# Moving the sample value pages, the sample value products and ten top-k rounds in a two-layer hybrid decoder step

## The reference, cut to what matters

```python
# layer 0, sample group: one query token for each of 8 samples, 1024 past positions + itself
score = einsum(relu(qi . idx_keys), wi) * IDX_SCALE      # indexer, 8 heads
_, idx = lax.top_k(score, 256)                           # prompt: top_k(score, 128) over <= 512 keys
k_sel, v_sel = gather from cache_k / cache_v by page_table (pages of 128 rows), new k, v for the last
logits = q . k_sel * ATTN_SCALE + t5_bias(table, dist)   # 16 heads, 4 KV heads
p = softmax(logits);  out = p . v_sel;  x = LN(ALPHA * x + out @ w_out)
# then a squared-ReLU MLP (4096), then layer 1: banded attention (window 128) with sinks, then an MLP
```

## Time and profile before

| what | value |
| --- | --- |
| median of 3 runs | 1299.87 us (1298.53 to 1301.01) |
| profiled execution, its own time | 1300.45 us |
| its span | 1298.8 us |
| PE busy | 1215.7 us (94%) |
| DVE busy | 708.2 us (55%) |
| ACT busy | 473.8 us (36%) |
| POOL busy | 102.0 us (8%) |

### The profile page before, as it was taken

One profiled execution on the slowest core, in us unless ns is written; L12 is line 12 of the kernel. 1 busy time (PEld: TensorE's weight loads), 2 busy tenths in 40 slices (PEclk: granted clock), 3 DMA queues, 4 the chain that ended last, 5 costly groups with the idle time before them and its releaser, 6 DMA issues.

```text
span 1298.8 us, 25590 instructions
## 1 busy us (share of the span) xinstructions
PE 1215.7 (94%) x9573; PEld 1113.3 (86%) x9573; DVE 708.2 (55%) x1440; ACT 473.8 (36%) x863; POOL 102.0 (8%) x139
## 2 busy tenths in 40 slices
PE   8999866999999999999999897889999999999995
PEld 4948723569999999999999896579999999999995
DVE  2289963766764343343357915957833433433477
ACT  2342214763452232231234426744531322322332
POOL 4333430000004000000000210000000000000000
PEclk9989968999999999999999998999999999999998
DMA  6645696002122222222223231012122222222221
GB/s 199 188 144 179 227 288 197 2 1 98 66 66 87 92 97 82 97 97 81 97 88 124 57 97 50 33 50 98 50 98 86 92 98 81 97 96 82 97 82 66
DMA packets 62155, 129.99 MB, mean 100 GB/s; under 512 B 9995, under 2 KB 34483, under 8 KB 61954
## 3 DMA queue, kind: packets, MB, share of 16 engines
q1 hardware_dynamic: 40978, 107.15, 24.3%
q10 hardware_dynamic: 14944, 13.91, 3.5%
q0 software_dynamic: 6160, 7.94, 2.2%
HBM read 124.35 MB, written 9.79 MB: 103 GB/s over the span
## 4 chain that ended last, share of the span: by engine, by line
PE 75%; DVE 16%; ACT 3%; SPq 3%; issue 3%; DMA 1%; POOL 0%; ACTq 0%; DVEq 0%
PE PS L541 59%; PE PS L571 6%; PE PS L761 2%; PE PS L721 2%; PE PS L708 2%; PE PS L735 2%; DVE YA L1521 2%; SPq L371 1%; DVE PB L1657 1%; SPq L362 1%; DVE YA L1508 1%; DVE PB L1682 1%; DVE RSTD L1513 1%; ACT PB L1133 1%; DVE X L1527 1%
## 5 line engine op out<-in xcount | busy, mean ns | idle before, releaser
L1364 DVE TENSOR_TENSOR WLO<-WRAW,WHI 128x1024 fp32r<-128x1024 f32 x118 | 145.3, 1232 | 352.5 <-ACT WHI L966 352.4
L966 ACT ACTIVATE WHI<-WRAW 128x1024 fp32r<-128x1024 f32 x126 | 133.5, 1060 | 404.2 <-PE PS L541 385.7
L541 PE MATMUL PS<-XH,WHI 128*128 128x260 f32 x1344 | 273.1, 284 | 1.9 <-DVE XL L1689 1.6
L541 PE MATMUL PS<-XH,WLO 128*128 128x260 f32 x1344 | 271.4, 284 | 0.0
L541 PE MATMUL PS<-XL,WHI 128*128 128x260 f32 x1344 | 270.8, 283 | 0.0
L541 PEld LDWEIGHTS PS<-XH,WHI 128*128 128x128 f32 x1344 | 207.7, 189 | 3.3 <-DVE XL L1689 2.3
L541 PEld LDWEIGHTS PS<-XH,WLO 128*128 128x128 f32 x1344 | 207.8, 189 | 0.0
L541 PEld LDWEIGHTS PS<-XL,WHI 128*128 128x128 f32 x1344 | 207.2, 189 | 0.0
L541 PE MATMUL PS<-HH,WHI 128*128 128x260 f32 x896 | 181.4, 283 | 0.2 <-DVE HL L1388 0.2
L541 PE MATMUL PS<-HH,WLO 128*128 128x260 f32 x896 | 180.6, 283 | 0.0
L541 PE MATMUL PS<-HL,WHI 128*128 128x260 f32 x896 | 180.3, 283 | 0.0
(11 more groups left out here) (268 smaller groups left out, 1732.1 us busy)
## 6 DMA issues: line engine op xcount, KB each, us to landing
WRAW<-wall SPq DMA_DIRECT2D x168, 512.0 KB, 3.2
bias_skewed<-bias_seq ACTq DMA_DIRECT2D x4, 1280.0 KB, 6.8
BT<-bias_skewed ACTq DMA_DIRECT2D x4, 1024.0 KB, 16.2
X<-xT SPq DMA_DIRECT2D x4, 520.0 KB, 7.2
X<-xT SPq DMA_DIRECT2D x1, 2080.0 KB, 10.2
yT<-X SPq DMA_DIRECT2D x8, 260.0 KB
KVB<-cacheK SPq DMA_DIRECT2D x16, 128.0 KB, 2.7
KVX<-cacheK SPq DMA_DIRECT2D x16, 128.0 KB, 3.0
```

Source lines behind the costliest of these rows:

```text
L541: mm = pe.matmul(PS[:, 2 * slot + g, 0:TG], w[:, slot, k, :], x[:, k, TG * g:TG * g + TG], start=(k == 0 and w is WHI and x is hi), stop=( ...
L966: nc.scalar.activation(WHI[:, slot], WRAW[:, slot], ACT.Copy).then_inc(hi_done, 1)
L1364: V.tensor_tensor(WLO[:, slot], WRAW[:, slot], WHI[:, slot].bitcast(F32), ALU.subtract).then_inc(lo_dve, 1)
```

## The change

It gives V pages their own places, brings the blocks of the prompt's masks and the first bias block elsewhere, and gives four queues a new order. PE does logits(0) and logits(1) of the prompt before the sample value products; the products move into the hook `sample_a(-1)`, their banks from 4 and 5 to 6 and 7, and the sample output's transposes to iteration 0, its copies (ACT and DVE) to iteration 1. DVE does 4 rounds (not 8) ahead of the query copies and 6 (not 5) behind them; the last ten stand between softmax_in(1) and normalise(0). The copies of the queries are cut in three, and the K logits run `gp` outermost, so that the first half needs the first four query units only. The new V row is multiplied straight out of `NAT` by an 8-row probability matrix that one more DVE operation (`DG`) and one matmul prepare. High and low parts of units 14 and 15 are made in iterations 3 and 4, since V pages stand in `WHI` and `WLO`. The digit matmuls sit one slot later each, the last three two slots later. Skewing the bias (four 1280 KB transfers) goes from ACT in units 8 to 11 to SP in the time of unit 5.

```diff
-KV_PLACE = (9, 10, 7, 8, 0, 1, 2, 3, 4, 5, 6, 9, 10, 7, 8, 11)
+KV_PLACE = (9, 10, 7, 8, 0, 1, 2, 3, 4, 5, 6, 12, 13, 11, 14, 9)
...
-KV_SPLIT = ((8, 8), (8, 8), (8, 8), (0, 8), (8, 8), (8, 8), (0, 8), (0, 8),
-            (4, 6), (4, 6), (4, 6), (5, 7), (5, 7), (5, 7), (5, 7), (4, 6))
-V_ORDER = (8, 9, 10, 15, 11, 12, 13, 14)
+KV_SPLIT = ((8, 8), (8, 8), (0, 0), (0, 8), (8, 8), (8, 8), (0, 8), (0, 8),
+            (4, 6), (4, 6), (4, 6), (4, 6), (8, 8), (4, 6), (4, 6), (4, 6))
+V_LATE = (8, 9, 10, 11, 13, 14, 15)
...
-SLOT_OF = (1, 2, 3, 4, 5, 6, 7, 8, 10, 11, 12)
+SLOT_OF = (2, 3, 4, 5, 6, 7, 8, 9, 12, 13, 14)
...
+        def load_values(eng, q, numbers):
+
+            eng.wait_ge(unit_done, A_OUT)
+            for n in V_LATE:
+                if kv_before(n):
+                    eng.wait_ge(kv_used, kv_before(n))
+                load_sample(eng, q, n, numbers)
...
+            early(POOL_LO[0] // 2, 0)
+            sp.wait_ge(toe_out, 16)
+            for i0 in range(0, P, 32):
+                sp.dma_start(bass.AP(tensor=bskew.tensor, offset=i0 * (NH * SKEW + 1),
+                                     ap=[[NH * SKEW + 1, 32], [SKEW, NH], [1, 640]]),
...
+            numbers = page_numbers(sp, 0, V_LATE)
+            early(POOL_LO[0] // 2, 1)
+            sp.wait_ge(toe_skew, 16 * 4)
+            sp.wait_ge(is_relu, 3 * IDXH)
             sp.wait_ge(ds_mm, 3)
-            with sp.Fori(0, NPG) as pg:
-                load_page(sp, 2, pg)
+            sp.dma_start(BT0[:], bskew[:, :, 127 + 384:127 + 512]).then_inc(toe_in[0], 16)
...
-            load_values(sp, 0)
+            sp.wait_ge(mask_done, 1)
+            sp.wait_ge(outs, 16 * 2)
+            with sp.Fori(0, NPG) as pg:
+                load_page(sp, 12, pg)
+            load_values(sp, 0, numbers)
             sp.wait_ge(kv_used, 2 * DB)
+            sp.wait_ge(toe_in[3], 16)
+            sp.wait_ge(lo_pool, LO_SKIP)
             for s in range(2):
                 load_unit(POOL_LO[1] + s, s)
...
-            with pool.Fori(0, NPG) as pg:
+            with pool.Fori(0, 4) as pg:
                 load_page(pool, 3, pg)
-            for u in range(*POOL_LO):
+            for u in range(POOL_LO[0], A_OUT):
                 low_part(u, u % 2)
...
+                if u < POOL_LO[0] + 4:
+                    load_page(pool, 3, 4 + u - POOL_LO[0])
+            load_values(pool, 1, numbers)
+            for u in range(A_OUT, POOL_LO[1]):
+                low_part(u, u % 2)
...
+            pe.wait_ge(ds_ev, 1)
+            for c0, c1 in spans:
+                pe.matmul(PSF[:, 2048 + c0:2048 + c1], TREP[:], ohd[:, c0:c1], start=True,
+                          stop=False)
             pe.wait_ge(qb_ready, 1)
...
+            for gp in range(2):
+                if gp:
+                    pe.wait_ge(qb_ready, 2)
+                for quad in (range(0, 4), range(4, 8)):
...
+            def sample_values():
+
+                pe.wait_ge(d_p, 1)
                 for k in range(NPG):
+                    pe.transpose(PS[:, 4 + k // 4, (k % 4) * P:(k % 4 + 1) * P],
+                                 PD[:, k * P:(k + 1) * P], ident)
+                pe.wait_ge(dg_done, 1)
...
                 if i == -1:
+                    sample_values()
+                if i == 0:
+                    pe.wait_ge(ov_ev, 2)
                     for q in range(2):
...
+                    numbers = page_numbers(act, 2, V_LATE)
...
-                high_part(u + 2, u % 2)
+                if u + 2 < A_OUT:
+                    high_part(u + 2, u % 2)
...
+                if 6 <= u < 8:
+                    with act.Fori(4 * (u % 2), 4 * (u % 2) + 4) as pg:
+                        load_page(act, 2, pg)
...
+            load_values(act, 2, numbers)
...
             act.wait_ge(d_mx, 1)
             nc.scalar.activation(PD[:], PD[:], ACT.Exp, bias=DST[:, 1:2],
                                  accum_out=DST[:, 2:3]).then_inc(d_exp, 1)
+            act.wait_ge(toe_skew, 16 * 4)
+            act.wait_ge(kv_used, DB)
+            load_bias(1)
...
                 if i == -1:
+                    for q in range(2):
+                        act.wait_ge(kv_used, DB + 4 * q + 4)
+                        nc.scalar.activation(OV[:, q, :], PS[0:112, 6 + q, 0:256], ACT.Copy
+                                             ).then_inc(ov_ev, 1)
+                    load_bias(2)
+                    load_bias(3)
+                if i in (3, 4):
+                    high_part(A_OUT + i - 3, i - 3)
+                if i == 1:
                     act.wait_ge(do_mm, 1)
...
-            prompt_rounds(8)
-            dve.wait_ge(ev_act, A_OUT)
...
+            prompt_rounds(4)
             dve.wait_ge(z_qb, 2)
...
+            dve.wait_ge(ev_act, 10)
+            queries(0, 4).then_inc(qb_ready, 1)
+            dve.wait_ge(ev_act, A_OUT - 1)
+            queries(4, 7)
+            dve.wait_ge(ev_act, A_OUT)
+            queries(7, 8).then_inc(qb_ready, 1)
+            prompt_rounds(6)
...
             prompt_rounds(1)
             sample_normalise(1, PD[:], False)
-            prompt_rounds(len(left))
+            dve.wait_ge(d_p, 1)
+            V.tensor_scalar(DG[:], ident, PD[:, 1024:1025], None, ALU.mult).then_inc(dg_done, 1)
 
             def sample_a(i):
 
                 if i == -1:
+                    prompt_rounds(len(left))
+                if i == 1:
                     dve.wait_ge(do_hi, 1)
```

More of the change, by code:

```diff
@@ L234, in program @@
         KID = place("KID", [P, 5, 2, HD])
+        KVZ = place("KVZ", [P, NPG, 256], at=kw)
         KIT = place("KIT", [P, TOK])
@@ L240, in program @@
         SC = place("SC", [P, 3, 512], at=ww)
+        MK12 = place("MK12", [P, 640], F32R, at=ww + 1536)
+        MK3 = place("MK3", [P, 512], F32R, at=hw + 7600)
         RS = place("RS", [P, 2, 512], at=ww + 1536)
@@ L277, in program @@
         DST = place("DST", [P, 4])
-        PNEW = place("PNEW", [1, P])
+        PNEW = place("PNEW", [DB, P])
         YS = place("YS", [P, TOK], at=rw)
@@ L386, in load_index_page, with page_numbers, load_sample @@
                           ).then_inc(done, 16)
-        def load_values(eng, q):
-            for group in (V_ORDER[:4], V_ORDER[4:]):
-                pages = {n: [page_number(eng, n, pg) for pg in range(*kv_pages(n)[q])]
-                         for n in group}
-                eng.wait_ge(unit_done, A_OUT)
-                for n in group:
-                    if n == 15:
-                        eng.wait_ge(lo_pool, LO_SKIP)
-                    if kv_before(n):
-                        eng.wait_ge(kv_used, kv_before(n))
-                    for pg, page in zip(range(*kv_pages(n)[q]), pages[n]):
-                        fetch_page(eng, n, pg, page)
+        def page_numbers(eng, q, samples):
+            return {n: [page_number(eng, n, pg) for pg in range(*kv_pages(n)[q])]
+                    for n in samples}
+        def load_sample(eng, q, n, numbers):
+            for pg, page in zip(range(*kv_pages(n)[q]), numbers[n]):
+                fetch_page(eng, n, pg, page)
+        def load_values(eng, q, numbers):
[4 more added lines that the diff above has]
+                load_sample(eng, q, n, numbers)
+        masks = (MK0[:], MK12[:, 0:256], MK12[:, 256:640], MK3[:])
         turns_a = Turns(lambda t: (0, t + 1))
@@ new lines, in sample_values @@
+            def sample_values():
+                pe.wait_ge(d_p, 1)
+                for k in range(NPG):
+                    pe.transpose(PS[:, 4 + k // 4, (k % 4) * P:(k % 4 + 1) * P],
+                                 PD[:, k * P:(k + 1) * P], ident)
+                pe.wait_ge(dg_done, 1)
+                pe.matmul(PS[0:DB, 6, 0:P], CST[:, C_SAM:C_SAM + DB], DG[:],
+                          start=True, stop=True).then_inc(dt_mm, 1)
+                pe.wait_ge(dt_ev, 1)
+                for b in range(DB):
+                    pe.matmul(sample_out(b), PNEW[:, NH * b:NH * b + NH],
+                              NAT[0:DB, 4, HD + IDXH:NATW], start=True, stop=False)
+                for quad in (range(0, 4), range(4, 8)):
+                    for b in quad:
+                        wait_kv(DB + b)
+                    for k in range(NPG):
+                        for b in quad:
+                            mm = pe.matmul(sample_out(b), PTD[:, k, NH * b:NH * b + NH],
+                                           kv_place(DB + b)[:, k, :], start=False,
+                                           stop=(k == NPG - 1))
+                            if k == NPG - 1:
+                                mm.then_inc(kv_used, 1)
```

157 lines of the change are left out of this document (61 added, 96 removed).

## The result

The changed kernel takes 1280.38 us (median of 4 runs, 1278.51 to 1280.54), the kernel before took 1300.44 beside it (4 runs, 1298.53 to 1302.15): a ratio of 0.9843 [0.9826, 0.9860], 20.1 us less. Forecast were 1275.0 us and 24.6 less, so the gain came, and 4.5 us of it are missing. The profiled executions say the same: spans of 1298.8 and 1278.8 us. From the start of unit 14 to the end both take 1004.3 us, so the whole difference lies ahead of it.

What follows compares the result with a forecast made beforehand. DMA engines (V pages), then an uncovered serial chain, were taken to set TensorE's first turn of probabilities. 30.7 - 0.6 - 5.5 = 24.6 us off 1300.45 gives 1275.9, predicted as 1275 us; forecast 1271 to 1278, range 1268 to 1283.

Steps and rivals of the forecast that it cites:

- Step 2: K logits on TensorE: start right behind unit 13 without idle at full clock, take 8.8 us, end at about 160.
- Step 5: Attention from first turn to unit 14: added work hands back 5.5 us, 3.2 of it a wait for the sample output's copies.
- step 3: VectorE's chain from the mask at 145.7 sets the next point: first probabilities scaled at 188.2, 30.7 us earlier.
- Step 4: Whether TensorE is free by the first scaling: V complete between 177 and 184, 0.6 us put on the path (bounds 0 and 5).
- step 1: Units 6 to 13 on TensorE with later digit slots: unit 13 ends near 150.3, 6.3 us earlier (bounds 4 and 7.5).
- the rival of the value path: V comes at 184 or later, with the bias load amid its pages: 1280 us (1278 to 1285), chance 0.18.
- unit 13 after 153: Sign on TensorE's timeline: unit 13 ending later than 153 us would make the units 6 to 13 estimate wrong.
- Count one of the two: VectorE's digit chain: one of two slow operations beside GpSimd's low parts assumed to go, some 2 us.
- a wait beyond 190: Sign on TensorE's timeline: waiting for V pages or a bias load beyond 190 us would make the prediction wrong.
- The rival of 150 GB/s: V pages and bias load run at half the rate seen: 10 us slower, 1310 us, chance 0.03.
- the 3 us more: Under the attention: by the exclusive port lock, VectorE's scalings and GpSimd's low parts exclude each other, sum some 3 us worse.
- the 30.7 us: First probabilities scaled by VectorE at 188.2 instead of 218.86 us: the gain before deductions.

Runs made afterwards that it cites:

- Experiment 5: The changed kernel with the digit matmuls back in their old slots (1 to 8, 10 to 12): 1281.45 us, ratio 0.9844 to the kernel before.
- Experiment 2: The changed kernel with SP reading V sample 12's page numbers ahead and issuing its eight pages straight, not in a loop: 1278.83 us.
- experiment 1: The changed kernel with ScalarE asking for the 2 MB of bias block 1 behind the first two exponentials instead of ahead of them: 1275.81 us.
- experiment 3: The changed kernel with VectorE taking the sample output's low part in iteration 2, between normalise(2) and softmax_in(4), instead of iteration 1: 1275.81 us.
- Experiment 4: The changed kernel with sample value products ahead of logits(0) again and the ten top-k rounds ahead of softmax_in(0): 1288.39 us.
- experiment 6: The changed kernel with high parts, and so low parts, of units 14 and 15 in iterations 6 and 7 instead of 3 and 4: 1281.07 us.
- 7: The changed kernel with GpSimd issuing the K page of unit 10's time ahead of that unit's low part instead of behind it: 1277.87 us.
- experiment 9: The changed kernel with the late bias load and the sample output's low part in iteration 2 together: 1273.32 us.

## Why the prediction was right or wrong, point by point

The mechanism was right in steps 2 and 5 and in the sum of step 3. Step 4 failed, and step 1 had the price of a meeting wrong. The sum was 4.6 us too large: unit 14 starts 19.96 us earlier instead of 24.6. Measured from the common point it starts 21.0 us earlier (196.3 and 175.3). The other 1.1 us are the later start of the whole stretch in this one execution (99.20 against 98.14); such starts scatter from 97.40 to 99.87 over kernels that are alike up to there, so this part isn't an effect that the runs can assign. What is left is 3.6 us: 3.1 by step 4 (3.7 less the 0.6 put there), 0.5 by step 3. That the time lies inside the range of 1268 to 1283 is in part luck: it missed the forecast's own 1271 to 1278, and fell where the rival of the value path, with a chance of 0.18, had put it.

**Step 1, units 6 to 13: the term was mis-sized.** Forecast 6.3 us earlier, measured 2.8 by the clock time (153.84 against 156.6), 3.8 from the common point (54.6 and 58.5). By the prediction's own sign, unit 13 after 153, this step is wrong, though only by the late start of this execution (98.14 + 54.6 would be 152.8). "Count one of the two" meetings was the count, and one long one came. But the sum gave it 1.2 us (7.5 for no meeting, 6.3 for one), and it cost TensorE 3.8 by the distances of the digits' matmuls: 5.28 us in front of 124.95 and 4.74 behind it, where 3.10 is the distance with nothing late. So 2.2 are waiting, and 1.6 the half unit at a granted clock of 0.57, which was not in the sum. As an estimate from these, unit 13 without any meeting would end 50.8 us behind the point, 7.7 earlier than before, near the bound of 7.5. The mask is ready at 149.14, where 145.7 was forecast. Experiment 5 shows that the 3.8 us belong to the slots, and that in the changed kernel unit 14 gets 2.1 of them, and the time no part that could be measured.

**Step 2, K logits: right.** They follow with no idle, at the full clock. They take 9.25 us, 153.84 to 163.09, where 8.8 were forecast; 0.3 of that is the K bias, 2.0 and not 1.7; that they end 3 us later than 160 is in the main step 1's miss.

**Step 3, VectorE sets the next point: its sum right, its claim wrong by one wait.** The first scaling ends at 189.77 against 188.2; from the common point 90.57 against 90.06 (188.2 - 98.14). sample_max waits for nothing, the ten rounds have no gap. That the sum fits is partly luck: the mask was 3.4 us late, and 1.5 of that were made up by a price that was too high. Six query copies took 1.14 us, where I had taken 2.6 from four in 1.70, and one of those four stood beside a low part of GpSimd (157.85 to 160.20) and took 1.09 alone, the others 0.19. But the scaling didn't set the first turn.

**Step 4, is TensorE free by then: this is the step that failed.** "I put 0.6 us for both on the path (bounds 0 and 5)": it was 3.7 (193.50 - 189.77). TensorE's wait for V ended at 182.7, inside of 177 to 184, so the sign named for this step, a wait beyond 190, didn't come. The error is in what stands behind the wait: I took only the second quad's products, 4.6 us. But the page that ended it was one of the first quad: SP's eight loop pages go first (10.66 us) and the first quad's last page stood behind them. So both quads' products came after the wait, 9.1 us, of which the first quad took 5.5 (the granted clock was 0.50 to 0.53 up to 187 us, behind 10.59 us of idling), with logits(2) behind them: 182.69 + 9.1 + 1.7 = 193.5. The last V page was there at about 185 (309 GB/s from 182.5 to 185, 54 from 185 to 187). Experiment 2 removes that order, and gains nothing, since then the last page is late; experiment 1 takes the 2 MB of bias out of the way and gains all of the 3.7 us. This is the rival "the value path decides", with its mechanism (the bias load in the middle of the pages), and close to its size (1280). Its other half didn't come: the two bias loads behind the products took ScalarE 2.50 us, not 7 each as in the full queues of the earlier trace rows. The rival of 150 GB/s is far from it, 344 GB/s in the window from 160 to 185.

**Step 5, handed back: right, 5.4 us against 5.5** (81.0 against 75.6). The hole in front of turn(2) is 3.24 us where 3.2 was forecast, and the turn behind it took 1.97 instead of 1.09; experiment 3 gives 3.1 us back. The low parts under the attention lengthen a scaling to 2.54 us and the negated maxima to 1.42, beside rows of the same shape of 1.14 and 0.17; of that TensorE sees 1.3 us of waiting at 217.97. The Trainium skill, SBUF — State Buffer, section "SBUF: two separate sides", gives the exclusive lock that such operations meet; the trace agrees in that the lengthened ones are those beside a low part, but not with the 3 us more that the prediction worked out from it: the total has no room for them.

**The order's share.** The prediction didn't split the 30.7 us. Experiment 4 does: 7 to 8 us by the order, 12 by the rest of the change.

## What to carry to other kernels

When a change takes away one wait, list everything that the next one holds back: not only when the last byte is there, but how much work stands behind the first byte that is late. A large load whose result is needed late shouldn't be asked for in the middle of many that are needed soon; moving it behind them gave 3.7 us for three lines. And a gain of one step is worth only what the latest of its neighbours lets through: the digit slots were 3.8 us for TensorE, nothing that could be measured in the time, and 3.3 us for VectorE, most of which (2.9, by medians that are near their noise) came through once the V pages no longer decided.

## What the runs showed of the hardware

- VectorE's operation of one column takes 0.16 us, and 2.31 where it begins 0.07 us behind a GpSimd subtraction: it ends at 123.38, the subtraction at 123.37. Each of the 13 profiled executions had one to three such meetings among the digits: one or two with the new slots, and with the old ones three (2.14, 0.96, and 3.31 us for the operation on `MSK`). Moving GpSimd's work moved the meeting with it (experiment 6) or put two shorter ones in its place (7), and one execution had two long ones where others, with the same work, had one. The rule of the exclusive lock (the Trainium skill, SBUF — State Buffer, section "SBUF: two separate sides") fits these ends.
- The granted clock, a mean over its window, was 0.57 for the 4 us behind a wait of TensorE of 1.95 us, and 0.52 for the 3.3 us behind one of 3.24 us (a turn of 1.97 us). It stayed at 1.00 behind waits of 0.82 and 1.30 us, and in experiment 9 also behind one of 1.94 us at the same place in the same work. So the length of a wait alone doesn't say whether the clock falls. Where it fell among the digits, the half unit took 4.74 us instead of 3.10, which is 1.6 us on top of the wait.
- The DMA engines moved 344 GB/s from 160 to 185 us, where the same stretch before the change had 278 and the earlier trace rows 294.
- A 2 MB bias load that ScalarE issued among V pages took 17.4 us to land and 0.6 us to issue; two of 1 MB issued into idle queues took 2.5 us to issue.
